# Leading conditioning group in four channel quarters instead of two halves, with four product tiles side by side in a four-layer transformer kernel

## The chip, the cores and the metric

One core of one Trainium2 chip. The metric is the device time of one execution in microseconds (us). The kernel before took 1589.12 us as the median of three runs (1589.05 to 1591.85).

## The reference

Two pairs of transformer layers run on 256 latent tokens (`x`) and 256 context tokens (`ctx`) of width 1024, all in fp32. Only the start matters here:

```python
sh1, sc1, g1, sh2, sc2, g2 = split(silu(c) @ w_ada[0] + b_ada[0], 6)   # the same for c_ctx
h  = rms_norm(x,   norm1_g[0]) * (1 + sc1)  + sh1                      # [256, 1024]
hc = rms_norm(ctx, norm1_g[0]) * (1 + csc1) + csh1                     # [256, 1024]
z, zc = h @ w_in[0], hc @ w_in[0]          # w_in[0]: [1024, 2048]; then attention, MLP, 3 more layers
```

## The kernel before, in words

Activations lie transposed: `X` holds 8 tiles of 128 channels ("k-tiles") by 512 token columns, 0 to 255 latent and 256 to 511 context. A product in fp32 is made of three matmuls on rounded parts: the weight block is split into `WHI` (ScalarE, `hi_split`) and `WLO` (VectorE, `lo_split`), the normalised activations into `HH` (ScalarE, in `norm_hi`) and `HL` (VectorE, `lo` inside `norm`). Weight blocks of 128 outputs by 8 k-tiles (512 KB) come through four `RAW` buffers; block n is in slot n % 4, is loaded when `lo_done` of block n-4 is reached, and is split when `blk_used` frees the slot's halves.

Every engine has its order written out by hand; semaphores join them. What matters is the start of layer 0:

- SyncE's queue loads `CST`, `VEC`, `MOD`, `CV`, `x`, `ctx` and then the first modulation group (`sh1` and `sc1`; 8 MB) into `MW` in six pieces (`PIECES`): two halves of the 1024 channels, each half in pieces of k-tiles 0-3, 4-5, 6-7, with weight blocks 0 to 3 laid between them.
- TensorE, in `first_blocks`, multiplies the conditioning vectors with each piece (`half_units`, line 2019: four matmuls side by side in four 32-column strips of the array), turns the result of a half to channel-major (`turn_half`), and runs product tiles 0 and 1 (`part`): each k-tile of a tile is three matmuls of 512 columns. In the first half it does k-tiles 0 and 1 of tile 0, between the pieces of the second half; the rest comes after the second half.
- VectorE adds a half to `MOD` and derives the scale `DER` (`mod_half`), then writes for each k-tile `NORM` = X * DER * RB (line 1337, two instructions) and `HL` (line 1322, two); ScalarE writes `HH` (line 800) between the two.
- The mean squares of the tokens are made by ScalarE (`first_squares`, one k-tile of 512 columns each) and VectorE (`accumulate`, seven additions), then `acc_sum` on TensorE.
- Tiles 2 and 3 (`products_tok`, weight blocks 2 and 3 side by side, lines 2000 to 2002) keep tokens on the output partitions: two token blocks, 8 k-tiles, three matmuls of 256 columns. They run one after the other in slots 2 and 3 of `proj(0)`. Slots 4 to 15 hold the next 12 tiles.
- The modulation groups 1 and 2 are 16 "units" of 1 MB (`mod_unit`, line 2008), one after each of slots 1 to 16. GpSimd loads them into two buffers, `GWA` and `GWB`, in turn (`unit`), the first two after the last piece of `MW` has landed, each later one when its buffer's last unit has been used.
- `tile_bank` gives tile i the PSUM bank i % 3. ScalarE empties the banks in `proj`, with a table load for Gelu ahead of tile 0's.

Of the kernel before, what the change touches and what calls it, by code (L numbers as in the profile page):

```python
# [161 lines left out]
def build(nc, A):  # L162
    ctx = ExitStack()
    with ctx:
# [48 lines left out]
        MW = sb("MW", [P, 2, KT, 4, 256], at=w0)  # L213
# [56 lines left out]
        vec_in, cst_in, x_in, ctx2_in, lam_in = sem("vec_in"), sem("cst_in"), sem("x_in"), sem("ctx2_in"), sem("lam_in")  # L270
        tab_in = [sem(f"tab_in{l}") for l in range(NLAYER)]
        raw_ready = [sem(f"raw_ready{s}") for s in range(4)]
        hi_done, lo_done, blk_used, drained = sem("hi_done"), sem("lo_done"), sem("blk_used"), sem("drained")
        mw_ready = [sem(f"mw_ready{c}") for c in range(6)]
        half_mm, half_ev, half_turn, half_add = sem("half_mm"), sem("half_ev"), sem("half_turn"), sem("half_add")
# [170 lines left out]
        def tile_bank(l, i):  # L446


            if IS_L[l] and i >= TPROJ[l] - 2:
                return banks[3 if i == TPROJ[l] - 2 else 2]  # L450
            return banks[i % 3]
# [74 lines left out]
        PIECES = [(0, 0, 4), (0, 4, 6), (0, 6, 8), (1, 0, 4), (1, 4, 6), (1, 6, 8)]  # L526
# [5 lines left out]
        def _(sp):  # L532
            sp.dma_start(CST[:], A["cst"]).then_inc(cst_in, 16)
            sp.dma_start(VEC[:], A["vec"]).then_inc(vec_in, 16)
            sp.dma_start(MOD[:].rearrange("p a b -> p (a b)"), A["bmod"]).then_inc(vec_in, 16)
            sp.dma_start(CV[:, 0:4 * KT], A["cvec"]).then_inc(cst_in, 16)
            sp.dma_start(X[:, :, 0:256], A["x"].rearrange("p (k t) -> p k t", k=KT)).then_inc(x_in, 16)
            sp.dma_start(X[:, :, 256:512], A["ctx"].rearrange("p (k t) -> p k t", k=KT)).then_inc(x_in, 16)
# [20 lines left out]
            for l in range(NLAYER):  # L559
                if l < 3:  # L560
                    base = sum(NPROJ[:l])
                    if l == 0:

                        for c, (h, k0, k1) in enumerate(PIECES):
                            r = 2 * h + k0 // 4
                            sp.dma_start(MW[:, h, k0:k1].rearrange("p a b c -> p (a b c)"),
                                         A["wmod0"][P * r:P * r + P, 1024 * (k0 % 4):1024 * (k0 % 4 + k1 - k0)]
                                         ).then_inc(mw_ready[c], 16)
                            for s in ([], [], [0], [1], [], [2, 3])[c]:
                                load(0, s, A["wproj"][s * P:s * P + P, :], 8)  # L570
# [26 lines left out]
        def _(gp):  # L597
# [71 lines left out]
            gp.wait_ge(mw_ready[5], 16)  # L669
# [48 lines left out]
        def _(act):  # L718
# [20 lines left out]
            def row_half(h):  # L739

                if h:
                    act.wait_ge(gb_done, 1)
                    act.wait_ge(half_turn, 1)
                else:
                    act.wait_ge(half_mm, 1)
                act_f(ROW[:, 256 * h:256 * h + 256], GB[:, 0:256], ACT.Copy).then_inc(gb_ev if h else half_ev, 1)

            def first_squares(kt):

                if kt == 0:  # L750
                    act.wait_ge(x_in, 32)
                if kt > 2:
                    act.wait_ge(acc_done, kt - 2)
                act_f(SQ[:, kt % 2, :] if kt else ACC[:], X[:, kt, :], ACT.Square).then_inc(acc_sq, 1)
# [33 lines left out]
            def norm_hi(key):  # L788
# [4 lines left out]
                for kt in range(KT):  # L793
                    if key == (0, "n1") and kt == 4:
                        hi_split(0, 1, 8)
                        row_half(1)
# [53 lines left out]
            def proj(l):  # L850
# [3 lines left out]
                for i in range(NSLOT[l]):  # L854
# [52 lines left out]
                    if (l, i) in ((0, 8), (0, 16)):  # L907
                        row_out({(0, 8): 1, (0, 16): 2}[l, i])
# [253 lines left out]
            for kt in range(KT):  # L1162
                first_squares(kt)
            roots((0, "n1"))
            hi_split(0, 0, 8)
            row_half(0)
            for l in range(NLAYER):
                norm((l, "n1"))
                if l == 0:
                    for s in (2, 3):  # L1170
                        hi_split(0, s, 8)
# [28 lines left out]
        def _(dve):  # L1200
# [28 lines left out]
            def mod_half(h):  # L1229


                dve.wait_ge(sel_done if h else half_turn, 1)
                t = MODP[:, 0:256].rearrange("p (q a b r) -> p a b q r", q=2, a=2, b=2)
                for part in range(2):
                    m = MOD[:, 8 * part + 4 * h:8 * part + 4 * h + 4, :].rearrange("p (b q) c -> p b q c", q=2)
                    ins = v.tensor_tensor(m, m, t[:, part, :, :, 0:2], ALU.add)
                ins.then_inc(mod_add if h else half_add, 1)
                dve.wait_ge(mod_add if h else half_add, 1)
                k = slice(4 * h, 4 * h + 4)
                link(v.scalar_tensor_tensor(out=DER[:, 0, k], in0=MOD[:, 8 + 4 * h:12 + 4 * h, :], scalar=1.0,  # L1240
                                            in1=vec(0, "g1", 4 * h, 4).unsqueeze(2).broadcast_to((P, 4, 2)),
                                            op0=ALU.add, op1=ALU.mult))

# [21 lines left out]
            def norm(key):  # L1265
# [61 lines left out]
                for kt in range(KT):  # L1327
                    if key == (0, "n1") and kt % 4 == 0:
                        if kt:
                            lo(3)  # L1330
                            lo_split(0, 1, 8)
                        mod_half(kt // 4)
# [8 lines left out]
                    if kt and not (key == (0, "n1") and kt == 4):  # L1341
                        lo(kt - 1)
# [36 lines left out]
            def proj(l):  # L1379
# [42 lines left out]
                for i in range(NSLOT[l]):  # L1422
# [33 lines left out]
                    if (l, i) == (0, 11):  # L1456
# [176 lines left out]
            def accumulate(l, which, m, a):  # L1633

                r, t = norm_after(l, which) if which else (0, 512)
# [283 lines left out]
            dve.wait_ge(vec_in, 32)  # L1919
            v.tensor_tensor(vec(3, "bpool", 0, KT), vec(3, "bpool", 0, KT), vec(3, "pscale", 0, KT), ALU.mult)  # L1920
            link(v.tensor_tensor(LPM[:], LP[:, :, 0:4:2, :], LP[:, :, 1:4:2, :], ALU.mult))
            for l in range(2):
                v.tensor_reduce(LAM[:, l, 0:2], LPM[:, l], AX.X, ALU.add).then_inc(lam_dots, 1)
            for l in range(2):
# [10 lines left out]
            for kt in range(1, KT):  # L1935
                accumulate(0, None, kt, kt % 2)
            roots(0, 4)
            lo_split(0, 0, 8)
            for l in range(NLAYER):
# [3 lines left out]
                if l == 0:  # L1943
                    for s in (2, 3):
                        lo_split(0, s, 8)
# [14 lines left out]
        def _(pe):  # L1960
# [31 lines left out]
            def products_tok(s, blocks, bank, qs):  # L1992

                w = P * blocks
                for j, q in enumerate(qs):
                    cols = slice(P * q, P * q + P)
                    out = bank[:, w * j:w * j + w].rearrange("p (a b) -> p a b", b=P)
                    for k in range(8):
                        wh, wl = WHI[:, s:s + blocks, k, :], WLO[:, s:s + blocks, k, :]
                        mm(out, HH[:, k, cols], wh, start=k == 0, stop=False)  # L2000
                        mm(out, HH[:, k, cols], wl, start=False, stop=False)
                        ins = mm(out, HL[:, k, cols], wh, start=False, stop=k == 7)
# [9 lines left out]
            def half_units(c):  # L2012


                h, k0, k1 = PIECES[c]
                pe.wait_ge(mw_ready[c], 16)
                for kt in range(k0, k1):
                    for j in range(4):
                        ins = mm(GB[32 * j:32 * j + 32, 0:256], CV[:, 4 * kt:4 * kt + 32], MW[:, h, kt, j, :],
                                 start=kt == 0, stop=kt == 7)  # L2020
                return ins

            def turn_half(h):

                pe.wait_ge(gb_ev if h else half_ev, 1)
                if h:
                    pe.wait_ge(half_add, 1)
                for q in range(2):
                    c = 256 * h + P * q
                    ins = nc.tensor.transpose(MODP[:, P * q:P * q + P], ROW[:, c:c + P], ident)  # L2030
                ins.then_inc(sel_done if h else half_turn, 1)

            def first_blocks():


                def part(b, ks, ready=None):
                    pe.wait_ge(lo_done, b + 1)
                    return products(b, 8, banks[b], 512, first=ks[0] == 0, stop=ks[-1] == 7, ready=ready, ks=ks)

                pe.wait_ge(cv_ready, 2)  # L2040
                half_units(0)
                acc_sum(0, 512)
                half_units(1)
                half_units(2).then_inc(half_mm, 1)
                norm_spread(0, 4)
                turn_half(0)
                half_units(3)
                part(0, [0, 1], (nl_ready, 0))
                half_units(4)
                half_units(5).then_inc(gb_done, 1)  # L2050
                turn_half(1)
                part(0, [2, 3], (nl_ready, 0))
                part(1, [0, 1, 2, 3])
                for k in range(4, 8):
                    for b in (0, 1):
                        ins = part(b, [k], (nl_ready, 0))
# [670 lines left out]
```

## Time and profile before

| | us |
|---|---|
| median of three runs | 1589.12 |
| the profiled execution | 1590.45 |
| its span, first to last instruction | 1588.4 |
| TensorE matmul busy | 1517.3 |
| TensorE's first matmul starts | 17.97 |
| first matmul of tile 4 starts | 62.40 |

The span is 2.05 us shorter than the profiled execution's time. In the timeline, PE is TensorE, PEld its weight loads, DVE VectorE, ACT ScalarE, POOL GpSimd and SPq the queue of SyncE. A matmul's duration holds its latency, so the distance between two starts says what one costs in a stream. A matmul on plain fp32 operands with 32 weight columns stands as two records.

### The profile page before, as it was taken

What the parts mean: (1) busy time and instruction counts of PE and PEld (TensorE: products, weight loads), DVE (VectorE), ACT (ScalarE), POOL (GpSimd) and SP (SyncE); (2) the same over time, 40 slices, a digit from 0 to 9 for tenths busy, and PEclk for the clock granted to TensorE, in tenths of its full rate; (3) what the DMA queues carried; (4) which work ended last, traced back from release to release, by engine and by line L of the source; (5) the groups of instructions that cost most, each with busy time, mean ns of one, the idle gap of its engine ahead of it and who ended that gap; (6) DMA issues with size and microseconds to landing.
All of it is one profiled execution on the core that took longest, in us unless ns stands there. A gap on an engine that the chain in (4) does not pass through costs nothing. (4 is left out here: it accounts for less than half of the span.)

```text
span 1588.4 us, 27175 instructions
## 1 busy us (share of the span) xinstructions
PE 1517.3 (96%) x9444; PEld 1268.4 (80%) x9444; DVE 1105.1 (70%) x1986; ACT 837.8 (53%) x1526; POOL 94.8 (6%) x160
## 2 busy tenths in 40 slices
PE   4999989999999999899899999999999998799997
PEld 2777667688888888887789998998788886488886
DVE  4464874798786477786678876774678855788865
ACT  3442882544444322465656665546566644566653
POOL 0111000110000011020000000000000000000000
PEclk9999999999999999999999999999999999899999
DMA  9775105665632488452067555542756587445563
GB/s 377 273 234 196 41 2 212 218 225 184 206 119 83 167 262 284 128 156 82 30 260 270 185 148 156 180 126 102 289 160 186 177 302 272 175 131 186 178 186 113
DMA packets 79685, 288.27 MB, mean 181 GB/s; under 512 B 9280, under 2 KB 12864, under 8 KB 71664
## 3 DMA queue, kind: packets, MB, share of 16 engines
q1 hardware_dynamic: 61056, 190.23, 37.8%
q0 software_dynamic: 18544, 96.90, 17.0%
q8 instruction: 54, 0.88, 0.2%
q14 instruction: 31, 0.25, 0.1%
HBM read 283.16 MB, written 1.05 MB: 179 GB/s over the span
## 5 line engine op out<-in xcount | busy, mean ns | idle before, releaser
L1213 DVE TENSOR_TENSOR WLO<-RAW,WHI 128x1024 fp32r<-128x1024 f32 (+1 forms) x376 | 412.2, 1101 | 154.3 <-ACT WHI L726 153.9
L726 ACT ACTIVATE WHI<-RAW 128x1024 fp32r<-128x1024 f32 (+1 forms) x376 | 357.0, 957 | 141.8 <-PE B L1973 86.5
L1971 PE MATMUL B<-HHL,WHI 128*128 128x256 f32 (+1 forms) x1184 | 397.8, 336 | 8.7 <-DVE HHL L1886 3.4
L1972 PE MATMUL B<-HHL,WHI 128*128 128x256 f32 (+1 forms) x1184 | 392.0, 331 | 0.0
L1973 PE MATMUL B<-HHL,WLO 128*128 128x256 f32 (+1 forms) x1184 | 391.9, 331 | 0.0
L1971 PEld LDWEIGHTS B<-HHL,WHI 128*128 128x128 f32 x1184 | 225.5, 190 | 42.2 <-issue 16.7
L1988 PE MATMUL B<-HHL,WHI 128*128 128x512 f32 x704 | 244.2, 400 | 1.7 <-DVE HHL L1322 1.7
L1973 PEld LDWEIGHTS B<-HHL,WLO 128*128 128x128 f32 x1184 | 225.6, 191 | 21.2
L1972 PEld LDWEIGHTS B<-HHL,WHI 128*128 128x128 f32 x1184 | 225.8, 191 | 19.6
L1986 PE MATMUL B<-HHL,WLO 128*128 128x256 f32 x704 | 184.4, 282 | 0.0
L1988 PE MATMUL B<-MID,WHI 128*128 128x512 f32 x462 | 163.5, 400 | 4.3 <-DVE WLO L1213 4.2
L1988 PEld LDWEIGHTS B<-HHL,WHI 128*128 128x128 f32 x704 | 127.7, 190 | 28.3 <-issue 3.8
L1986 PEld LDWEIGHTS B<-HHL,WLO 128*128 128x128 f32 x704 | 133.9, 190 | 8.0
L1986 PE MATMUL B<-MID,WLO 128*128 128x256 f32 x462 | 126.1, 280 | 0.0
L1988 PEld LDWEIGHTS B<-MID,WHI 128*128 128x128 f32 x462 | 85.7, 188 | 26.7 <-DVE WLO L1213 6.0
L1679 DVE SCALAR_TENSOR_TENSOR Y<-B,VEC,Y 128x510 f32<-128x510 f32 (+1 forms) x88 | 54.0, 614 | 57.7 <-ACT Y L1074 45.8
L1971 PE MATMUL B<-MID,WHI 128*128 128x512 f32 (+1 forms) x264 | 91.3, 346 | 0.5 <-DVE WLO L1213 0.5
L1972 PE MATMUL B<-MID,WHI 128*128 128x512 f32 (+1 forms) x264 | 91.0, 345 | 0.0
L1973 PE MATMUL B<-MID,WLO 128*128 128x512 f32 (+1 forms) x264 | 91.0, 345 | 0.0
L1067 ACT ACTIVATE Y<-Y 128x256 f32<-128x256 f32 (+1 forms) x88 | 41.5, 472 | 90.0 <-DVE Y L1704 47.1
L1986 PEld LDWEIGHTS B<-MID,WLO 128*128 128x128 f32 x462 | 87.2, 189 | 1.8
L1078 ACT ACTIVATE MID<-Y 128x256 f32 (+3 forms) x88 | 41.5, 472 | 82.8 <-DVE Y L1722 53.4
(266 smaller groups left out, 2183.4 us busy)
## 6 DMA issues: line engine op xcount, KB each, us to landing
RAW<-in_wup SPq DMA_DIRECT2D x176, 512.0 KB, 3.7
GWR<-in_wmod POOLq DMA_DIRECT2D x27, 1024.0 KB, 8.0
RAW<-in_wdn SPq DMA_DIRECT2D x64, 384.0 KB, 3.2
RAW<-in_wproj SPq DMA_DIRECT2D x44, 512.0 KB, 4.6
RAW<-in_wdn SPq DMA_DIRECT2D x64, 320.0 KB, 3.2
WDU<-in_wdot POOLq DMA_DIRECT2D x32, 512.0 KB, 5.0
WDD<-in_wdot POOLq DMA_DIRECT2D x32, 512.0 KB, 4.8
GWA<-in_wmod POOLq DMA_DIRECT2D x15, 1024.0 KB, 5.9
```

The costliest lines, as they stand in the source:

```text
L726: act_f(WH[s][:, 0:kts, :], RAW[s][:, 0:kts, :], ACT.Copy).then_inc(hi_done, 1)
L1067: act_f(yg, yg, ACT.Silu).then_inc(silu_done, 1)
L1078: act_f(mid, yv if isinstance(i, int) else Y[:, 2 * j + 1:2 * j + 2, 0:t], ACT.Copy).then_inc(mid_hi, 1)
L1213: v.tensor_tensor(WL[s][:, 0:kts, :], RAW[s][:, 0:kts, :], WH[s][:, 0:kts, :].bitcast(F32), ALU.subtract).then_inc(lo_done, 1)
L1679: v.scalar_tensor_tensor(out=y[:, :, 1:256], in0=b[:, :, 0:255], scalar=w(0, which), in1=y[:, :, 1:256], op0=ALU.mult, op1=ALU.add).then_i ...
L1971: mm(bank[:, 0:t], wh, a, start=first and k == ks[0], stop=False)
L1972: mm(bank[:, 0:t], wh, b, start=False, stop=False)
L1973: ins = mm(bank[:, 0:t], wl, a, start=False, stop=stop and k == ks[-1])
L1986: ins = mm(bank[:, 0:256], WL[s][:, k, :], T[:, 0, k0 + k, 0:256], start=False, stop=False)
L1988: ins = mm(bank[:].rearrange("p (a b) -> p a b", a=2), WH[s][:, k, :], T[:, :, k0 + k, 0:256], start=first and k == 0, stop=end)
```

## The change

The first group comes in four quarters of 256 channels (two k-tiles), each in two pieces of 1 MB; weight blocks 0 to 3 are all loaded after the first quarter. `x` and `ctx` move ahead of `VEC` and `MOD`, each with a semaphore of its own, and are squared and added per half of the tokens. All four tiles are open at once (tile 3 in bank 3): each quarter's two k-tiles are multiplied into all four. Units 0 and 1 of group 1 move behind tile 3, units 2 to 13 follow slots 4 to 15, and units 14 and 15 stand in slot 16. The diff, cut to its core:

```diff
-        PIECES = [(0, 0, 4), (0, 4, 6), (0, 6, 8), (1, 0, 4), (1, 4, 6), (1, 6, 8)]
+        PIECES = [(c // 2, 4 * (c % 2)) for c in range(8)]
 # SyncE: CST, CV, X latent (x_in), X context (ctx_in), VEC, MOD, then
-                            for s in ([], [], [0], [1], [], [2, 3])[c]:
+                            for s in range(4) if c == 1 else ():
                                 load(0, s, A["wproj"][s * P:s * P + P, :], 8)
 # GpSimd
-                    if l == 0 and 1 <= i < 15:
-                        unit(1 + (i + 1) // 8, (i + 1) % 8)
+                    if l == 0 and 2 <= i < 16:
+                        unit(1 + i // 8, i % 8)
-            gp.wait_ge(mw_ready[5], 16)
+            gp.wait_ge(mw_ready[7], 16)
 # ScalarE
+            def row_part(q):
+                act.wait_ge(part_mm, q + 1)
+                if q:
+                    act.wait_ge(part_turn, q)
+                act_f(ROW[:, P * q:P * q + P], GB[:, 0:P], ACT.Copy).then_inc(gb_ev if q == 3 else part_ev, 1)
+            def first_squares(n):
+                half, c = n // 4, n % 4
+                j = 3 * half + c - 1
+                if c == 0:
+                    act.wait_ge(ctx_in if half else x_in, 16)
+                elif j >= 2:
+                    act.wait_ge(acc_done, j - 1)
+                out = Y[:, 2 + half, :] if c == 0 else Y[:, j % 2, :]
+                act_f(out..., X[:, 2 * c:2 * c + 2, 256 * half:256 * half + 256], ACT.Square).then_inc(acc_sq, 1)
 # norm_hi
+                    if key == (0, "n1") and kt in (2, 4, 6):
+                        row_part(kt // 2)
                     act.wait_ge(nt_ready, base + kt + 1)
 ...
+                    if key == (0, "n1") and kt == 1:
+                        for s in (1, 2, 3):
+                            hi_split(0, s, 8)
 # before norm:
+            row_part(0)
             hi_split(0, 0, 8)
-            row_half(0)
 # VectorE
+            def mod_part(q):
+                dve.wait_ge(sel_done if q == 3 else part_turn, 1 if q == 3 else q + 1)
+                ... v.tensor_tensor(m, m, t, ALU.add); wait; DER[:, 0, 2q:2q+2] as in mod_half
+            def first_sums(half):
+                acc = Y[:, 2 + half, :]
+                for c in range(1, 4):
+                    ... v.tensor_tensor(acc, acc, Y[:, j % 2, :], ALU.add).then_inc(acc_done, 1)
+                ins = v.tensor_tensor(acc[:, 0:256], acc[:, 0:256], acc[:, 256:512], ALU.add)
 # norm
-                    if key == (0, "n1") and kt % 4 == 0:
+                    if key == (0, "n1") and kt % 2 == 0:
                         if kt:
-                            lo(3)
-                            lo_split(0, 1, 8)
-                        mod_half(kt // 4)
+                            lo(kt - 1)
+                        for s in (1, 2, 3) if kt == 2 else ():
+                            lo_split(0, s, 8)
+                        mod_part(kt // 2)
+                        if kt == 0:
+                            lo_split(0, 0, 8)
 # TensorE
+            def part_units(q):
+                if q:
+                    pe.wait_ge(part_ev, q)
+                for c in (2 * q, 2 * q + 1):
+                    pe.wait_ge(mw_ready[c], 16)
+                    for kt in range(PIECES[c][1], PIECES[c][1] + 4):
+                        for j in range(4):
+                            ins = mm(GB[32 * j:32 * j + 32, 0:P], CV[:, 4 * kt:4 * kt + 32], MW[:, q, kt, j, :],
+                                     start=kt == 0, stop=kt == 7)
+                ins.then_inc(part_mm, 1)
 # first_blocks; wide(b, k): k-tile k of tile b, after lo_done b+1 and nl_ready k+1;
 # tok(tile, k): the same for tiles 2 and 3, after lo_done 4; both(k): wide(0, k), wide(1, k)
+                pe.wait_ge(acc_done, 7); ...four sums of the squares
+                part_units(0); norm_spread(0, 4); turn_part(0)
+                wide(0, 0); wide(0, 1); wide(1, 0); wide(1, 1)
+                part_units(1); tok(2, 0); tok(2, 1); turn_part(1)
+                tok(3, 0); tok(3, 1); both(2); both(3)
+                part_units(2); tok(2, 2); turn_part(2)
+                tok(2, 3); tok(3, 2); tok(3, 3); both(4)
+                part_units(3); both(5); turn_part(3)
+                tok(2, 4); tok(3, 4); tok(2, 5); tok(3, 5)
+                both(6); both(7); tok(2, 6); tok(2, 7); tok(3, 6); tok(3, 7)
 # proj
-                    if l == 0 and 1 <= i < 17:
-                        mod_unit(1 + (i - 1) // 8, (i - 1) % 8)
+                    if l == 0:
+                        for u in (0, 1) if i == 3 else (14, 15) if i == 16 else [i - 2] if i > 3 else ():
+                            mod_unit(1 + u // 8, u % 8)
```

The turn of group 1 and what follows it move one slot later (`row_out`, `mod_turn`, `mod_apply`).

## Rows read from the trace of the kernel before

**Rows 1.** Page, part 1: busy us (share of the span) xinstructions.
```profile
PE 1517.3 (96%) x9444; PEld 1268.4 (80%) x9444; DVE 1105.1 (70%) x1986; ACT 837.8 (53%) x1526; POOL 94.8 (6%) x160
```
**Rows 2.** Waits, 0 to 45 us: us in total, times, longest.
```profile
PE B L2019 <- DMA MW<-in_wmod: 21.1, 2, 18.0
```
**Rows 3.** DMA issues at 37 and 62 us: count, KB each, us to landing.
```profile
GWA<-in_wmod POOLq DMA_DIRECT2D x1, 1024.0 KB, 8.2
...
GWA<-in_wmod POOLq DMA_DIRECT2D x1, 1024.0 KB, 5.2
```
**Rows 4.** Timeline, 12 to 48 us: start, us, engine, line, operation [idle before].
```profile
12.97 0.63 ACT L754 ACTIVATE ACC<-X 128x512 f32<-128x512 f32 x1 [5.67 <-DMA X<-in_ctx]
...
14.24 5.47 DVE L1639 TENSOR_TENSOR ACC<-ACC,SQ 128x512 f32<-128x512 f32 x7 [5.58 <-ACT SQ L754]
...
17.97 3.46 PE L2019 MATMUL B<-MW,CV 128*32 128x256 f32 x32 [17.97 <-DMA MW<-in_wmod]
...
21.36 1.05 PE L2087 MATMUL B<-CST,ACC 128*128 128x1 f32 x8
...
22.34 1.93 PE L2019 MATMUL B<-MW,CV 128*32 128x256 f32 x32
...
46.51 1.28 ACT L881 ACT_TABLE_LOAD   x1
47.81 0.60 ACT L881 ACTIVATE AU<-B 128x512 f32<-128x512 f32 x1
```
**Rows 5.** Timeline, 25 to 30 us, from the row copy to the second half's units.
```profile
25.07 0.36 ACT L746 ACTIVATE ROW<-B 128x256 f32<-128x256 f32 x1
25.27 1.23 DVE L1213 TENSOR_TENSOR WLO<-RAW,WHI 128x1024 fp32r<-128x1024 f32 x1 [2.35 <-ACT WHI L726]
25.49 0.44 PE L2030 MATMUL B<-CST,ROW 128*128 128x128 f32 x2 [0.64 <-ACT ROW L746]
26.41 0.23 DVE L1236 TENSOR_TENSOR MOD<-MOD,B 128x8 f32<-128x8 f32 x2
...
26.87 1.66 DVE L1337 SCALAR_TENSOR_TENSOR NORM<-X,DER,B 128x256 f32<-128x256 f32 x4
...
28.72 0.88 DVE L1322 SCALAR_TENSOR_TENSOR HHL<-NORM,MOD,HHL 128x256 fp32r<-128x256 f32 x2 [0.19 <-ACT HHL L800]
...
29.04 3.64 PE L2019 MATMUL B<-MW,CV 128*32 128x256 f32 x32 [3.11 <-DMA MW<-in_wmod]
```
**Rows 6.** Timeline of TensorE, 46 to 63 us: starts of products and units.
```profile
46.07 0.39 PE L1971 MATMUL B<-HHL,WHI 128*128 128x512 f32 x1
...
46.75 0.39 PE L1971 MATMUL B<-HHL,WHI 128*128 128x512 f32 x1
...
47.52 1.07 PE L2008 MATMUL B<-GWA,CV 128*32 128x512 f32 x8
48.52 0.39 PE L2000 MATMUL B<-WHI,HHL 128*128 128x256 f32 x1
...
54.47 1.06 PE L2008 MATMUL B<-GWB,CV 128*32 128x512 f32 x8
...
62.40 0.50 PE L1971 MATMUL B<-HHL,WHI 128*128 128x512 f32 x1
```
**Rows 7.** The same timeline at 144 us: two strips, 128 columns, 8 pairs.
```profile
144.07 1.09 PE L2183 MATMUL B<-WST,AV 128*64 128x128 f32 x16
```
**Rows 8.** TensorE by stretch: window, us, busy (x), granted clock, DMA share, GB/s.
```profile
28.00:29.00 1.00, 0.00 (x0) 0.50 1.08 446
...
34.00:35.00 1.00, 1.00 (x4) 0.62 0.98 397
...
713.00:714.00 1.00, 0.42 (x2) 1.00 0.69 254
714.00:715.00 1.00, 1.00 (x5) 0.51 0.83 318
```
**Rows 9.** Waits of TensorE, 660 to 720 us: us in total, times, longest.
```profile
PE B L2000 <- DVE WLO L1213: 3.4, 2, 1.9
```

More of the change, by code:

```diff
@@ L273, in build @@
         hi_done, lo_done, blk_used, drained = sem("hi_done"), sem("lo_done"), sem("blk_used"), sem("drained")
-        mw_ready = [sem(f"mw_ready{c}") for c in range(6)]
-        half_mm, half_ev, half_turn, half_add = sem("half_mm"), sem("half_ev"), sem("half_turn"), sem("half_add")
+        mw_ready = [sem(f"mw_ready{c}") for c in range(8)]
+        part_mm, part_ev, part_turn, part_add = sem("part_mm"), sem("part_ev"), sem("part_turn"), sem("part_add")
         gw_ready = {k: sem(f"gw_ready_{k}") for k in GW}
@@ L562, in _ @@
                     if l == 0:
[L564 to L568, printed above, removed]
[L569 removed]
+                        for c, (q, k0) in enumerate(PIECES):
+                            sp.dma_start(MW[:, q, k0:k0 + 4].rearrange("p a b c -> p (a b c)"),
+                                         A["wmod0"][P * q:P * q + P, 512 * k0:512 * k0 + 2048]).then_inc(mw_ready[c], 16)
+                            for s in range(4) if c == 1 else ():
                                 load(0, s, A["wproj"][s * P:s * P + P, :], 8)
@@ L737, in row_out @@
                 act_f(ROW[:], GB[:], ACT.Copy).then_inc(gb_ev, 1)
[L739 to L754, printed above, removed]
+            def row_part(q):
[11 more added lines that the diff above has]
+                out = Y[:, 2 + half, :] if c == 0 else Y[:, j % 2, :]
+                act_f(out.rearrange("p (a b) -> p a b", a=2), X[:, 2 * c:2 * c + 2, 256 * half:256 * half + 256],
+                      ACT.Square).then_inc(acc_sq, 1)
             def late_squares(key, c):
@@ L1161, in _ @@
                 act_f(LAM[:, l, 0:2], LAM[:, l, 0:2], ACT.Exp).then_inc(lam_exp, 1)
-            for kt in range(KT):
-                first_squares(kt)
+            for n in range(8):
+                first_squares(n)
             roots((0, "n1"))
+            row_part(0)
             hi_split(0, 0, 8)
-            row_half(0)
             for l in range(NLAYER):
                 norm((l, "n1"))
-                if l == 0:
-                    for s in (2, 3):
-                        hi_split(0, s, 8)
                 if l < 3:
@@ L1227, in mod_apply @@
                 dve.wait_ge(mod_add, turn_place(g) + 1)
[L1229 to L1241, printed above, removed]
-                                            op0=ALU.add, op1=ALU.mult))
+            def mod_part(q):
+                dve.wait_ge(sel_done if q == 3 else part_turn, 1 if q == 3 else q + 1)
+                m = MOD[:, 0:16, :].rearrange("p (a k) c -> p a k c", a=2)[:, :, 2 * q:2 * q + 2, :]
+                t = MODP[:, 0:P].rearrange("p (a e r) -> p a e r", a=2, e=2)[:, :, :, 0:2]
+                v.tensor_tensor(m, m, t, ALU.add).then_inc(mod_add if q == 3 else part_add, 1)
+                dve.wait_ge(mod_add if q == 3 else part_add, 1 if q == 3 else q + 1)
+                link(v.scalar_tensor_tensor(out=DER[:, 0, 2 * q:2 * q + 2], in0=MOD[:, 8 + 2 * q:10 + 2 * q, :], scalar=1.0,
+                                            in1=vec(0, "g1", 2 * q, 2).unsqueeze(2).broadcast_to((P, 2, 2)),
+                                            op0=ALU.add, op1=ALU.mult))
@@ new lines, in first_sums @@
+            def first_sums(half):
+                acc = Y[:, 2 + half, :]
+                for c in range(1, 4):
+                    j = 3 * half + c - 1
+                    dve.wait_ge(acc_sq, 4 * half + c + 1)
+                    if j:
+                        dve.wait_ge(acc_done, j)
+                    v.tensor_tensor(acc, acc, Y[:, j % 2, :], ALU.add).then_inc(acc_done, 1)
+                dve.wait_ge(acc_done, 3 * half + 3)
+                ins = v.tensor_tensor(acc[:, 0:256], acc[:, 0:256], acc[:, 256:512], ALU.add)
+                if half:
+                    ins.then_inc(acc_done, 1)
+                else:
+                    link(ins)
@@ L1340, in norm @@
                     ins.then_inc(nt_ready, 1)
-                    if kt and not (key == (0, "n1") and kt == 4):
+                    if kt and not (key == (0, "n1") and kt % 2 == 0):
                         lo(kt - 1)
@@ L1633, in accumulate @@
             def accumulate(l, which, m, a):
-                r, t = norm_after(l, which) if which else (0, 512)
+                r, t = norm_after(l, which)
                 dve.wait_ge(acc_sq, 8 * EARLY[r] + m + 1)
@@ L1923, in _ @@
                 v.tensor_reduce(LAM[:, l, 0:2], LPM[:, l], AX.X, ALU.add).then_inc(lam_dots, 1)
+            for half in range(2):
+                first_sums(half)
+            dve.wait_ge(vec_in, 32)
+            v.tensor_tensor(vec(3, "bpool", 0, KT), vec(3, "bpool", 0, KT), vec(3, "pscale", 0, KT), ALU.mult)
             for l in range(2):
@@ L1934, in _ @@
             dve.wait_ge(lam_ready, 2)
-            for kt in range(1, KT):
-                accumulate(0, None, kt, kt % 2)
             roots(0, 4)
-            lo_split(0, 0, 8)
             for l in range(NLAYER):
@@ L1990, in products_apart, with products_tok @@
                 return ins
-            def products_tok(s, blocks, bank, qs):
+            def products_tok(s, blocks, bank, qs, ks=None):
                 w = P * blocks
@@ L1997, in products_tok @@
                     out = bank[:, w * j:w * j + w].rearrange("p (a b) -> p a b", b=P)
-                    for k in range(8):
+                    for k in ks or range(KT):
                         wh, wl = WHI[:, s:s + blocks, k, :], WLO[:, s:s + blocks, k, :]
-                        mm(out, HH[:, k, cols], wh, start=k == 0, stop=False)
-                        mm(out, HH[:, k, cols], wl, start=False, stop=False)
-                        ins = mm(out, HL[:, k, cols], wh, start=False, stop=k == 7)
+                        mm(out, HH[:, k, cols], wh, start=k == 0 and not (ks and j), stop=False, skip_group_check=bool(ks))
+                        mm(out, HH[:, k, cols], wl, start=False, stop=False, skip_group_check=bool(ks))
+                        ins = mm(out, HL[:, k, cols], wh, start=False, stop=k == 7, skip_group_check=bool(ks))
                 return ins
@@ L2010, in mod_kt @@
                 return ins
[L2012 to L2031, printed above, removed]
+            def part_units(q):
[8 more added lines that the diff above has]
+                ins.then_inc(part_mm, 1)
@@ L2033, in first_blocks, with turn_part, wide @@
+            def turn_part(q):
+                if q == 3:
+                    pe.wait_ge(gb_ev, 1)
+                else:
+                    pe.wait_ge(part_ev, q + 1)
+                if q:
+                    pe.wait_ge(part_add, q)
+                nc.tensor.transpose(MODP[:, 0:P], ROW[:, P * q:P * q + P], ident).then_inc(
+                    sel_done if q == 3 else part_turn, 1)
             def first_blocks():
-                def part(b, ks, ready=None):
+                def wide(b, k):
@@ L2050, in first_blocks @@
[L2050 to L2056, printed above, removed]
-                        if k == 7:
-                            ins.then_inc(blk_used, 1)
+                    ins = products(b, 8, banks[b], 512, first=k == 0, stop=k == 7, ready=(nl_ready, 0), ks=[k])
@@ new lines, in wide, with tok, both @@
+                    if k == 7:
+                        ins.then_inc(blk_used, 1)
+                def tok(tile, k):
+                    T = TILES[0][tile]
+                    pe.wait_ge(lo_done, 4)
+                    pe.wait_ge(nl_ready, k + 1)
+                    ins = products_tok(2, 2, tile_bank(0, tile), T["qs"], ks=[k])
+                    if k == 7:
+                        ins.then_inc(*((blk_used, 2) if T["last"] else (tile_mm, 1)))
+                def both(k):
+                    wide(0, k)
+                    wide(1, k)
@@ new lines, in first_blocks @@
+                pe.wait_ge(cv_ready, 2)
+                pe.wait_ge(acc_done, 7)
+                for q in range(4):
+                    ins = mm(STAT[:, q:q + 1], Y[:, 2 + q // 2, P * (q % 2):P * (q % 2) + P], cst("ones"), start=True,
+                             stop=True)
+                ins.then_inc(stat_mm, 1)
+                part_units(0)
+                norm_spread(0, 4)
+                turn_part(0)
+                for b in range(2):
+                    for k in range(2):
+                        wide(b, k)
@@ new lines, in first_blocks @@
+                part_units(1)
+                tok(2, 0)
+                tok(2, 1)
+                turn_part(1)
+                tok(3, 0)
+                tok(3, 1)
+                both(2)
+                both(3)
+                part_units(2)
+                tok(2, 2)
+                turn_part(2)
+                tok(2, 3)
+                tok(3, 2)
+                tok(3, 3)
+                both(4)
+                part_units(3)
+                both(5)
+                turn_part(3)
+                for k in (4, 5):
+                    tok(2, k)
+                    tok(3, k)
@@ L2060, in mod_unit @@
+                for k in (6, 7):
+                    both(k)
+                for tile in (2, 3):
+                    for k in (6, 7):
+                        tok(tile, k)
             def mod_unit(g, kt):
@@ L2210, in proj @@
                         pair()
-                    if 2 <= i < TPROJ[l] - IS_L[l] or l == 2 and i == 1:
+                    if (2 if l else 4) <= i < TPROJ[l] - IS_L[l] or l == 2 and i == 1:
                         tile = 2 if l == 2 and i == 1 else i
```

38 lines of the change are left out of this document (11 added, 27 removed).

## The prediction, on record before the changed kernel ran

> **What bounds the kernel now.** I read the page's first part, then TensorE's waits, then the timeline of the first 65 us. TensorE is busy 96% of the span [rows 1], and the change touches only its start: what matters is when the tile of slot 4 begins, and how much unit work is behind TensorE by then. From there to the weave it waits for nothing but one row copy, and every slot keeps its order. At the start TensorE waits 21.1 us for pieces of `MW` in two waits [rows 2]: 18.0 us for the first, then 3.1 us for the second half, which arrives at 29.04 [rows 5]. In the second wait the clock falls to 0.50, the lower level of 1.2 GHz; it is back between 34 and 35 us [rows 8]. After that the stretch to 62.40 is nearly solid, with three units (0, 1, 2) in it [rows 6]. So 62.40 is the mark: the change gains or loses what the same work ends earlier or later than that.
>
> **What the pieces cost.** Three numbers come first.
> A product's k-tile in tiles 0 and 1 costs 46.75 - 46.07 = 0.68 us [rows 6]; at half clock 1.36. In tiles 2 and 3 it costs (54.47 - 48.52 - 0.2) / 8 = 0.72 us; the 0.2 is the gap ahead of the unit. Interleaving the four tiles adds no instruction: 2 x 8 x 0.68 + 2 x 8 x 0.72 = 22.4 us either way.
> The conditioning product of a quarter has 32 matmuls of 128 columns, where a half had 32 of 256: twice as many in all. Before, 32 records (16 matmuls, eight groups of four strips) took 1.93 us, latency of the last included, so about 0.22 us a group [rows 4]. The 128-column form with 32-column strips does not stand in the trace. Two-strip groups of 128 columns do: eight pairs in 1.09 us, or (1.09 - 0.2) / 8 = 0.11 us a pair [rows 7]. If the time goes with the columns streamed, a quarter is 16 groups x 0.11 = 1.8 us; if with the records, as in that row, 64 x 1.09 / 16 = 4.4 us. I take 1.8, since both rows give half the time for half the columns; at half clock it is 3.6. The upper end would add 2.6 us for each quarter behind the first.
> The Trainium skill (TensorE: Matmul & The Clock Gate, "Back-to-back issue gap") says that pairs of weight load and matmul at N = 128 sustain only about 81 ns each, which would be 5.2 us a quarter and 10 us more for the three; the row of before stands at 54 ns a record and that of two strips at 68, so the trace does not bear it out.
>
> **Until the first product.** The first quarter is 2 MB in the queue's same place as the first piece before, so it is there at about 17.9 [rows 4]. `ctx` was there at 12.97 [rows 4]; 0.53 MB of `VEC` and `MOD` leave its way, at 400 GB/s 1.3 us, so 11.6. Behind it ScalarE squares (0.6 each), VectorE adds three times 0.78 (5.47 / 7) and folds for 0.5: 15.5; sums on TensorE 1.05, so 16.6. The units' first half fills 16.6 to 18.4 at half clock, as the first 32 records did (3.46 against 1.93) [rows 4], the second half ends at 20.2. That the squares come first is thus worth little: TensorE would be free to start at 17.9 in any case. Then the chain: row copy 0.36, turn 0.4, which with the spread ahead of it makes 21.5; `mod_part` 0.46 (26.41 to 26.87); `lo_split` of block 0, which now stands between `mod_part` and the norms, 1.23; norms of two k-tiles 1.66; the wait for ScalarE 0.19 and the first `HL` 0.88 [rows 5]. First product at 25.9 or 26.0, where it was 32.6. The weight blocks (2 MB) are in by 23.
> TensorE idles 4.5 us before it, longer than the 3.1 after which it went to 0.50 before, so I let it be at 0.50 from here for the four wide k-tiles.
>
> **The four quarters on TensorE.** Each quarter has a chain of its own: turn ended, `mod_part` 0.46, norms 1.66, 0.19, `HL` 0.88: 3.2 us to the next product that can run. Beside it TensorE has what the order puts behind the turn.
> - Four wide k-tiles at half clock, 5.4: 31.4. Units of quarter 1, 1.8: 33.2. Two tok 1.44, turn 0.2: 34.9. Behind the turn only tile 3's two k-tiles, 1.44: 36.3. Chain: 35.1 + 3.2 = 38.3. Stall 2.0.
> - Four wide 2.7: 41.0. Units 1.8: 42.8. One tok, turn: 43.8. Three tok 2.16: 45.9. Chain: 44.0 + 3.2 = 47.2. Stall 1.3.
> - Two wide 1.36, units 1.8, two wide 1.36, turn: 51.9. Four tok 2.9: 54.8. Chain 55.3. Stall 0.5.
> - Four wide 2.7, four tok 2.9: 60.9. Units 0 and 1 of group 1, 2.07 (47.52 to 48.52 is one) [rows 6]: 63.0. Slot 4 starts.
> The three `lo_split` of blocks 1 to 3 (26.9 to 30.5) fit beside the first four wide tiles and the units. The last piece of 9 MB lands near 38, before its units at 48.5, so DMA no longer binds from 26 on.
> Slot 4's own wait: block 4 can be split once tile 0 ends at 57.5. ScalarE has its table 1.28 behind it, Gelu 0.60 [rows 4], hi 1.0, VectorE 1.23 [rows 5]: 60.5. The four tok and two units cover it to 63.0; without them it would cost 2.4.
> **The sum.** Before, three units were done at 62.40; now two at 63.0, and the third (1.0) is still due in slot 16, where nothing hides it: 63.0 + 1.0 - 62.4 = +1.6 us. The 14 units left do the same work as before. Unit 2's load is issued when unit 0 has used the buffer, at 62.1, and is needed after slot 4's product at 68.5: 6.4 us, against landings of 5.2 to 8.2 [rows 3]: 0 to +1.8, I take 0, since the long one stood in the crowded start. The squares' seven adds, now six and two folds, lie beside the DMA; one turn more in four, and DER in quarters, are in the chains above. The profiled execution would be 1590.45 + 1.6 = 1592.1 (span 1590.0); on the median of 1589.12 the same shift gives **1590.7**.
>
> **The rivals.**
> *The clock falls in a stall* (slower). TensorE now has gaps of 2.0 and 1.3 us among narrow unit matmuls. Elsewhere a microsecond at 0.42 busy was followed by one at 0.51 of the clock [rows 8], yet a wait of 1.9 us was not [rows 9]. The fall at the start lasted from 28 to past 34, 6.6 us [rows 8], which costs 3.3; one half as long costs 1.7, and I take that. One fall gives +3.3, 1592.4; with unit 2's load late by 1.8 as well, +5.1, 1594.2. It decides when one falls and the sum is not too high elsewhere.
> *Quarters fully hidden* (faster). If the 3.2 us chain lay wholly beside products, the stalls (3.8) go: -2.2; and if the clock also rises before the first wide tiles, -2.7 more: -4.9, 1584.2. For it: TensorE has products to do 6.6 us earlier. Against it: the order puts 1.4 us behind the first turn, and VectorE's instructions are known rows.
> *Only the clock is better.* It rises 2 to 3 us earlier than I let it: 1590.7 - 1.3 = 1589.4, no change that can be told.
> *The narrow matmuls don't halve.* 3 x 2.6 = +7.8, less what the stalls take up of it (nothing, as the chain starts behind them): 1598.5. Against it [rows 4, 7].
> *The change does nothing in effect*, as a gain at the start is lost at slot 4: that is within the forecast.
>
> **How the numbers follow.** A measurement of this kernel can tell about 0.2%, 3.2 us: faster is under 1585.9, slower over 1592.3. My forecast, with the clock case beside it, holds 0.50 (all no change). Clock fall, alone or with the late unit: 0.27, nearly all of it just over the bound. Narrow matmuls: 0.05. Quarters hidden, wholly or with a start chain shorter than I have it: 0.18, of which 0.15 pass the bound. That makes faster 0.15, same 0.53, slower 0.32. The range runs from 1587.0 (half of the stalls hidden, clock up early) to 1594.5 (one fall and a late unit).
>
> **What would show it.** Right: first product (line of `wide`) near 26; waits of TensorE on `HL` of about 2.0, 1.3 and 0.5 us, and no wait for `MW` after the first quarter; a quarter's 64 records in about 1.9 us; slot 4 near 63.0; everything after it shifted by the same amount. Wrong: a slot 4 start before 60 (stalls absent or clock up), a granted clock of 0.50 again between 36 and 50, a wait for `GWA` after slot 4, or a quarter over 3 us.

## The result, and the profile after

The changed kernel takes 1600.83 us (median of six runs, 1596.18 to 1602.78) against 1589.7 for the kernel before in the same runs: ratio 1.0065, interval 1.0051 to 1.008. A forecast of +1.6 us met +11.1. The profiled execution took 1600.62 us, its span 1598.5.

The rows of after stand in the order of the forecast's steps. The page's first part, for [rows 1]:
```profile
PE 1524.4 (95%) x9572; PEld 1277.9 (80%) x9572; DVE 1105.6 (69%) x1989; ACT 837.5 (52%) x1528; POOL 94.8 (6%) x160
```
TensorE is busy for 7.1 us more and the span is 10.1 longer, so part of the loss stands in matmuls (128 records more, and slower ones) and part is waiting. The waits of TensorE in the first 75 us (us in total, times, longest), where [rows 2] had 21.1 us for `MW`:
```profile
PE B L2074 <- DVE Y L1253: 14.9, 1, 14.9
PE B L1985 <- DVE HHL L1337: 8.0, 4, 4.5
PE B L2022 <- DMA GWA<-in_wmod: 1.8, 1, 1.8
```
No wait for `MW` is left. L2074 makes the sums of the squares, and L2022 is a unit. L1985 is the first matmul of a wide k-tile (one of tiles 0 or 1, 512 columns), and its four waits are the gap ahead of the first product and the three stalls. The last line is unit 2, whose load took nearly as long as the crowded one of [rows 3]:
```profile
GWA<-in_wmod POOLq DMA_DIRECT2D x1, 1024.0 KB, 7.9
```
The timeline of the same stretch (L2035 is a quarter's units):
```profile
14.90 1.84 PE L2074 MATMUL B<-CST,Y 128*128 128x1 f32 x8 [14.90 <-DVE Y L1253]
16.67 3.64 PE L2035 MATMUL B<-MW,CV 128*32 128x128 f32 x64
...
22.07 1.23 DVE L1214 TENSOR_TENSOR WLO<-RAW,WHI 128x1024 fp32r<-128x1024 f32 x1
23.21 1.65 DVE L1355 SCALAR_TENSOR_TENSOR NORM<-X,DER,B 128x256 f32<-128x256 f32 x4
...
26.09 0.77 PE L1985 MATMUL B<-HHL,WHI 128*128 128x512 f32 x1 [4.51 <-DVE HHL L1337]
...
31.48 2.21 PE L2035 MATMUL B<-MW,CV 128*32 128x128 f32 x64
...
38.73 0.63 PE L1985 MATMUL B<-HHL,WHI 128*128 128x512 f32 x1 [1.88 <-DVE HHL L1337]
...
43.23 1.95 PE L2035 MATMUL B<-MW,CV 128*32 128x128 f32 x64
...
49.52 0.47 PE L1985 MATMUL B<-HHL,WHI 128*128 128x512 f32 x1 [1.17 <-DVE HHL L1337]
...
58.04 0.47 PE L1985 MATMUL B<-HHL,WHI 128*128 128x512 f32 x1 [0.45 <-DVE HHL L1337]
...
65.66 0.50 PE L1985 MATMUL B<-HHL,WHI 128*128 128x512 f32 x1
...
73.17 1.06 PE L2022 MATMUL B<-GWA,CV 128*32 128x512 f32 x8 [1.78 <-DMA GWA<-in_wmod]
```
The first product is at 26.1 (forecast 26.0), the stalls are 1.9, 1.2 and 0.45 us (2.0, 1.3, 0.5), and a quarter of units at full clock takes 1.95 with its latency. The product behind the first stall shows the main thing that differs up to here: it is slow. TensorE by stretch (window, us, busy, granted clock, DMA share, GB/s), to set beside [rows 8]:
```profile
37.00:38.00 1.00, 0.00 (x0) 1.00 1.02 406
38.00:39.00 1.00, 0.27 (x1) 0.94 1.03 410
39.00:40.00 1.00, 1.00 (x3) 0.50 1.03 410
...
42.00:43.00 1.00, 1.00 (x5) 0.85 1.02 413
...
160.00:161.00 1.00, 0.00 (x0) 1.00 0.94 295
161.00:162.00 1.00, 0.78 (x8) 0.88 0.95 401
162.00:163.00 1.00, 0.68 (x4) 0.50 0.99 418
```
Beside the stretch that the forecast had, from 25.2 to 32.0 us, the clock is at its lower level (1.2 GHz) twice in the first 175 us: for 3.4 us behind the 1.9 us stall, and for 6.8 us from 161.8 on. What stands ahead of that second fall is slot 16, the place the forecast did not work out. TensorE:
```profile
157.19 1.06 PE L2022 MATMUL B<-GWA,CV 128*32 128x512 f32 x8
161.22 1.46 PE L2022 MATMUL B<-GWB,CV 128*32 128x512 f32 x8 [2.97 <-DMA GWB<-in_wmod]
```
and GpSimd, which issues the load that it waits for:
```profile
155.97 0.53 POOL L604 DMA_DIRECT2D GWB<-in_wmod  x1 [6.46 <-PE B L2022]
```
The load took 5.2 us, and unit 15 could have run at 158.2. Before, the last unit's buffer was free at 143.5, 8.6 us ahead of the unit, which ran with no wait:
```profile
143.88 0.53 POOL L605 DMA_DIRECT2D GWB<-in_wmod  x1 [2.38 <-PE B L2008]
152.09 1.06 PE L2008 MATMUL B<-GWB,CV 128*32 128x512 f32 x8
```

**Where the time went.** VectorE's 376 weight splits have the same order in both kernels, so the difference of their starts shows how late the changed kernel is at each point:

| split of | before, us | after is later by | what lies between |
|---|---|---|---|
| block 7 | 64.2 | 2.4 | |
| block 8 | 70.3 | 3.2 | slot 4 |
| block 9 | 80.2 | 5.1 | the wait for `GWA`, 1.8 |
| block 16 | 134.3 | 5.0 | slots 6 to 13 |
| block 17 | 165.6 | 11.9 | slot 16 and the start of the attention behind it (the weave) |
| the last | 1572.2 | 10.2 | the other layers |

Between blocks 16 and 17 stand the unit more in slot 16 (1.0), the wait (3.0) and the half clock behind it (the remaining 2.9). Of the 1.7 given back later, 1.5 lie between 690 and 747 us, where the clock of before fell [rows 8] and that of the changed kernel did not. Later falls move the difference to and fro: it is 11.6 at 1262 us, 7.9 at 1374 and 10.2 from 1416 on.

### The profile page after: what moved, and what is told of

Read it like the earlier page. It is cut to its first block and busy times, and to the rows that moved or that the text cites. A ratio compares the mean times of both kernels' runs of the same rounds, so it can differ in the third digit from the quotient of the medians.

```text
span 1598.5 us, 27467 instructions
## 1 busy us (share of the span) xinstructions
PE 1524.4 (95%) x9572; PEld 1277.9 (80%) x9572; DVE 1105.6 (69%) x1989; ACT 837.5 (52%) x1528; POOL 94.8 (6%) x160
## 3 DMA queue, kind: packets, MB, share of 16 engines
HBM read 283.16 MB, written 1.05 MB: 178 GB/s over the span
## 5 line engine op out<-in xcount | busy, mean ns | idle before, releaser
L1985 PE MATMUL B<-HHL,WHI 128*128 128x256 f32 (+1 forms) x1184 | 398.3, 336 | 15.6 <-DVE HHL L1337 10.6
L1985 PEld LDWEIGHTS B<-HHL,WHI 128*128 128x128 f32 x1184 | 225.5, 190 | 48.8 <-issue 24.8
L1985 PE MATMUL B<-MID,WHI 128*128 128x512 f32 (+1 forms) x264 | 91.4, 346 | 0.5 <-DVE WLO L1214 0.5
```

What stands on the lines that cost most here:

```text
L1985: mm(bank[:, 0:t], wh, a, start=first and k == ks[0], stop=False)
```

## The experiments

A ratio is against runs of the kernel before that stood beside the kernel's own: 1589.81 for e1 to e4, 1589.39 for e5 to e8, 1590.2 for e9 to e11. Most medians are of 11 or 12 runs, that of e3 of six and that of e8 of five. "Filler" is a row of matmuls of 128 columns whose results nobody reads. "Behind before" is always the difference of the starts of the same weight split in the two profiled executions.

| run | median, us | ratio to before, interval |
|---|---|---|
| e1, units put back | 1590.02 | 1.0008, 0.9993 to 1.0023 |
| e2, before with late units | 1594.13 | 1.0031, 1.0017 to 1.0044 |
| e3, changed, with filler | 1597.38 | 1.0044, 1.0029 to 1.006 |
| e4, quarters one ahead | 1586.65 | 0.9979, 0.9968 to 0.9991 |
| e5, e4 with filler | 1585.96 | 0.9975, 0.9963 to 0.9987 |
| e6, e2 with filler | 1594.44 | 1.0027, 1.0013 to 1.004 |
| e7, e4, tables first | 1589.68 | 0.9999, 0.9984 to 1.0014 |
| e8, changed, again | 1600.24 | 1.006, 1.0038 to 1.0083 |
| e9, e4 and 1.75 us | 1589.62 | 0.9998, 0.9988 to 1.0009 |
| e10, e4 and 3.5 us | 1591.16 | 1.0008, 0.9997 to 1.002 |
| e11, before and 1.75 us | 1591.18 | 1.0008, 0.9998 to 1.0018 |

**e1, the units put back.**
```diff
 # GpSimd, ScalarE, VectorE: loads, row copy and use of the units as in the kernel before
 # first_blocks
                 tok(2, 4); tok(3, 4); tok(2, 5); tok(3, 5)
+                mod_unit(1, 0)
                 both(6); both(7)
+                mod_unit(1, 1)
 # proj
-                    if l == 0:
-                        for u in (0, 1) if i == 3 else (14, 15) if i == 16 else [i - 2] if i > 3 else ():
-                            mod_unit(1 + u // 8, u % 8)
+                    if l == 0 and 3 <= i < 17:
+                        mod_unit(1 + (i - 1) // 8, (i - 1) % 8)
```


> The changed kernel, with the unit schedule of the kernel before: unit 0 behind the last turn, unit 1 behind tiles 0 and 1, unit 2 behind tile 3, then one unit a slot. Theory U (most of the loss is unit loads that come due one slot after they are issued, and the clock fall behind the last of them): the waits for GWA (1.8 us) and GWB (3.0) go, and with them the fall to 0.50 at 162 us (about 3.3) - some 8 us faster than the changed kernel, about 1592 to 1594, 3 us over the kernel before. Rival F (the loss is made in the first 65 us, the rest only passes it on): within 2 us of the changed kernel, 1599 to 1601.


It is 10.8 us faster than the changed kernel (10.2 by e8), more than theory U said; rival F falls. Its waits of TensorE in the first 100 us:
```profile
PE B L2074 <- DVE Y L1253: 14.9, 1, 14.9
PE B L1985 <- DVE HHL L1337: 7.6, 3, 4.5
```
Of the stalls of the quarters, those of 1.89 and 1.17 us are still there and unit 0 fills the third; no buffer is waited for, and the clock does not fall at 162. Nor does it after the 1.9 us stall:
```profile
36.00:37.00 1.00, 0.18 (x2) 1.00 0.99 401
37.00:38.00 1.00, 0.00 (x0) 1.00 1.00 401
38.00:39.00 1.00, 0.94 (x4) 1.00 1.08 430
39.00:40.00 1.00, 1.00 (x6) 1.00 1.03 410
```
So theory U holds for the two waits and the fall behind the second; of the surplus, the traces give 1.7 to the fall at 39 us, which e1's execution does not have, and 0.45 to the third stall. By the weight splits e1 is 1.9 us behind before from 63 to 134 us: that is what the front part of the change costs with no such fall and the third stall filled.

**e2, only the late units.** The kernel before with the lines that e1 takes out, put in.


> The kernel before, with only the unit schedule of the change: units 0 and 1 in slot 3, units 2 to 13 in slots 4 to 15, units 14 and 15 in slot 16, loads and turn of the group to match. Theory U: a wait for GWB of 2 to 3 us in slot 16, one for GWA of 0 to 2 us in slot 4, a clock fall at the weave: +5 to +8 us, 1595 to 1598. Rival F: +0 to +2 us.


+4.3 us, a little under theory U's range; F falls again. Its waits of TensorE, 100 to 175 us:
```profile
PE B L2008 <- DMA GWB<-in_wmod: 3.2, 1, 3.2
```
and the clock is at 0.50 from 154.5 to 161.3. Between blocks 16 and 17 it loses 7.0 us, like the changed kernel (6.9). There was no wait for `GWA` in slot 4; that one stands only in kernels that have the change's front as well (the changed kernel, e3, e8).

**e3, filler in the idle times.**
```diff
+                def warm_pe(n):
+                    for _ in range(n):
+                        mm(STAT[:, 128:256], ident, CST[:, 0:128], start=True, stop=True)
                 turn_part(0)
+                warm_pe(20)
...
+                warm_pe(7)
                 both(2)
...
+                warm_pe(4)
                 both(4)
```


> The changed kernel, with matmuls of 128 columns whose results nobody reads in three of its idle times: 20 ahead of the first product, 7 ahead of k-tile 2, 4 ahead of k-tile 4. Theory C (idle TensorE, not the narrow matmuls, brings the clock down): no 0.50 between 25 and 43 us, slot 4 starts 3 to 4.5 us earlier than its 65.7, and the whole is about that much faster than the changed kernel. Rival (the narrow unit matmuls bring it down): the clock falls as before, and the time is the same or up to 1 us longer.


Theory C holds: no 0.50 between 22 and 158 us, slot 4 at 61.9 instead of 65.7, and 3.4 us less in the median (2.9 by the e8 runs). Slot 4 starts with:
```profile
61.94 0.50 PE L1985 MATMUL B<-HHL,WHI 128*128 128x512 f32 x1
```
Narrow unit matmuls alone did not bring the clock down. The saving holds the half clock ahead of 32 us too, which the forecast had counted in. The wait in slot 16 (2.9) and a fall behind it (3.4 us) stayed.

**e4, each quarter one ahead.**
```diff
 # first_blocks, units as in e1
-                wide(0, 0); wide(0, 1); wide(1, 0); wide(1, 1)
-                part_units(1); tok(2, 0); tok(2, 1); turn_part(1)
-                tok(3, 0); tok(3, 1); both(2); both(3)
-                part_units(2); tok(2, 2); turn_part(2)
-                tok(2, 3); tok(3, 2); tok(3, 3); both(4)
-                part_units(3); both(5); turn_part(3)
+                wide(0, 0); wide(0, 1); part_units(1); wide(1, 0); turn_part(1); wide(1, 1)
+                tok(2, 0); tok(2, 1); tok(3, 0); tok(3, 1)
+                part_units(2); both(2); turn_part(2); both(3)
+                tok(2, 2); tok(2, 3); tok(3, 2); tok(3, 3)
+                part_units(3); both(4); turn_part(3); both(5)
```


> The changed kernel with the unit schedule of before and with each quarter's conditioning matmuls and turn put ahead of the products of the quarter before it, so that its chain through VectorE and ScalarE lies beside products. Theory S (the stalls come from the place of the turn, with only 1.4 to 2.9 us of products behind it against a chain of 3.2): the stalls of about 2.3, 1.2 and 0.5 us go, and so does the clock fall in the first of them (1.9); 5 to 6 us less than with the units alone put back, about 1587 to 1588, which is 1 to 3 us under the kernel before. Rival (VectorE's own work, 3.5 us of weight splits and 3.4 a quarter, is the bound): within 2 us of the version with the units put back.


Theory S holds in kind: the stalls are gone, and only the gap ahead of the first product is left (waits of TensorE, 12 to 100 us):
```profile
PE B L2074 <- DVE Y L1253: 14.9, 1, 14.9
PE B L1985 <- DVE HHL L1337: 4.5, 1, 4.5
```
It is 3.4 us under e1 (the stalls of 3.1 us; there was no fall to save) and 3.2 under the kernel before, with an interval that lies under 1. It beats both kernels, though by less than the 5 to 6 us under e1 that were expected.

**e5, and a filler ahead of the first product** (`warm_pe(16)` behind `turn_part(0)`).


> The version with the units put back and the quarters one ahead, with 16 matmuls of 128 columns (results not read) between the first turn and the first product, where TensorE idles 4.5 us and the clock falls at 24.3 us. Theory C: the clock stays up through the first products, which saves 1.4 us in two wide k-tiles, 1.2 in the units and 0.7 in the next, less up to 0.5 if the filler ends late: 2 to 3 us faster, about 1584. Rival (VectorE's three weight splits from 26.5 to 30 us then bind the second tile): 0 to 1 us.


In the trace the clock stays at 1.00 where e4 has 0.50 from 24.3 to 31.1 (the same window in e5 and in e4):
```profile
28.00:29.00 1.00, 1.00 (x44) 1.00 1.05 434
```
```profile
28.00:29.00 1.00, 1.00 (x10) 0.50 1.03 426
```
and block 8's split is 2.0 us earlier, with no wait for a weight split. The median is 0.7 lower, which is the rival's number, and the intervals can't tell the two kernels apart. The gain is shown for the place, not for the whole.

**e6, filler in the wait of slot 16** of e2: 15 such matmuls between units 14 and 15 (`+` lines in `proj`, line 2243).


> The kernel before with the late unit schedule (4.3 us slower than before in the median), and 15 matmuls of 128 columns whose results nobody reads between units 14 and 15, in the wait for GWB. Theory W (of the 7 us lost in slot 16, 3.2 are the wait, 1.0 the unit, and about 3 the half clock that the wait brings): no fall to 0.50 at 155 us, 2.5 to 3.5 us faster than without the filler, 1590.5 to 1592. Rival (the fall comes from the narrow matmuls of the weave itself): no gain, 1594 to 1595.


The fall at the weave is gone with nothing but the filler added, so the idle time did bring it:
```profile
151.20 3.62 PE L2243 MATMUL B<-CST 128*128 128x128 f32 x30
155.36 1.07 PE L2008 MATMUL B<-GWB,CV 128*32 128x512 f32 x8 [0.55 <-DMA GWB<-in_wmod]
```
Blocks 16 to 17 lose 5.2 us instead of 7.0; it would be about 4.3, but this execution's load took 6.3 us where e2's took 5.5. The median did not follow (1594.44 against 1594.13), and by that number the rival fits: theory W holds for the place and not for the whole time. In the two profiled executions e6 is 2.0 us ahead of e2 at block 17 and 0.4 behind it at the last split: its clock is at half for 34.1 us between 1300 and 1405, that of e2 for 23.9. One execution of each can't say whether that is chance, so why the median stays is open.

**e7, tables first.**
```diff
             sp.dma_start(CST[:], A["cst"]).then_inc(cst_in, 16)
+            ...VEC, MOD
             ...CV, x, ctx
-            ...VEC, MOD
```


> The version with the quarters one ahead, with the load order of before (VEC, MOD and CV ahead of the tokens). Theory: the token sums are late by 1.3 us, the first half of the conditioning matmuls starts that much later, and the second half, which waits for its piece until 17.9 anyway, by 0.9: first product and the whole 0.5 to 1 us later, 1587 to 1588, hardly to be told. Rival (the tokens first matter as much as the rest): 2 us or more.


The base is e4. In the trace the sums start 0.9 us later, the first product 0.65, and block 8 is 0.3 later than in e4. The median is 3.0 higher, the rival's number and far more than the trace's front accounts for; with an interval of about 2.4 us on either side it is inconclusive. In its profiled execution e7 is 0.9 us ahead of e4 at 1330 us and 3.1 behind it at 1416, again with 34.1 us at half clock between 1300 and 1405 against 23.9.

**e8, the changed kernel again.**


> The changed kernel once more, beside the others on this chip. If the fall of the clock at 39 us belongs to the 2 us stall there, it can be missing in one execution and present in another, as the version with the units put back had the same stall of 1.9 us and no fall. Waits for GWA of 1 to 2 us and for GWB of 3 us and the fall at the weave are expected every time; median 1598 to 1602.


All as expected: the same waits (1.89, 1.17, 0.45; `GWA` 1.8, `GWB` 3.0), and the clock falls at 38.4 and 161.3. So with this order it fell behind the first stall in both profiled executions, and with e1's, which is the same up to there, it did not.

**e9, e10, e11, a plain shift.**
```diff
                 for i in range(NSLOT[l]):
+                    if (l, i) == (0, 4):
+                        for _ in range(8):        # 16 in e10
+                            mm(MODP[:, 0:P], ident, CST[:, 0:P], start=True, stop=True)
```


> The version with the quarters one ahead, plus 8 matmuls of 128 columns (results not read; 1.75 us by their rate of 0.22 each) ahead of slot 4, with TensorE at full clock. Everything behind is only shifted. Theory K (all that follows passes a shift on unchanged): 1586.65 + 1.75 = 1588.4, within 0.7. Rival P (the short falls of the clock later in the kernel stand at times of their own, so a shift moves the gaps of 700 to 1400 us in or out of them): the median moves by another amount than 1.75, by up to 3 us.

> The same with 16 such matmuls, a shift of 3.5 us. Theory K: 1586.65 + 3.5 = 1590.1, within 0.7. Rival P: off by up to 3 us, and not in line with the shift of 1.75.

> The kernel before with 8 such matmuls ahead of slot 4, a shift of 1.75 us, about that by which the version with the units put back is late there (1.9), though its median is only 0.2 to 0.3 us over that of before. Theory K: +1.75, 1591.3. Rival P: the shift is given back in part by later falls of the clock, as in that version: 0 to +1 us.


In the traces the shifts stand at block 8 as put in: 1.7, 3.6 and 1.8 us. Each against its own runs of before, the median of e4 moved from -3.2 to -0.6 and +1.0, so by 2.6 and 4.2 where 1.75 and 3.5 were put in; that of before moved by 1.0 where 1.75 was. On medians theory K is good to about 1 us, not to the 0.7 it gave itself. Rival P is not ruled out: with intervals of about 1.7 us on either side, e11's +1.0 fits both. For single executions P is what the traces show: e10's span was 1587.2 and e9's 1589.6, with 1.75 us more work in e10, since e9 had 13.6 us more of half clock behind 600 us.

## Why the prediction was wrong

The time of the first product and the three stalls were right to 0.2 us each. In the first there is some luck: the sums of the squares started at 14.90, where the forecast has 15.5, and took 1.84 us instead of 1.05. The narrow conditioning matmuls take half the time, as forecast (1.8 us a quarter; 1.95 with its latency measured). The Trainium skill (TensorE: Matmul & The Clock Gate, "Back-to-back issue gap") gives about 81 ns a matmul with its weight load at N = 128; 64 records in 1.95 us, 0.2 of latency off, are 27 ns each, or 55 for a matmul of two records, so for strips side by side the measurement lies below it.

The step that failed is in the sum: "the third (1.0) is still due in slot 16, where nothing hides it" and "the 14 units left do the same work as before". The work is the same, but not the distance between a buffer's release and its next use. Two buffers alternate, so unit 15 needs the buffer of unit 13. Unit 13 had moved to the end of slot 15, and slot 16 has no product: 2.3 us lie between the issue of the load (155.97) and the time of use (158.2), and the load needs 5.2. The forecast works out unit 2's margin and not the other place where two units stand together, so it puts this wait at nothing without a reason. The price in the trace was 3.0 for the wait and 2.9 for the half clock behind it, which e6's trace ties to the wait. That the unit schedule is the cause is shown both ways: e2 puts it into the kernel before, with a wait of 3.2, and e1 takes it out.

The rival "the clock falls in a stall", given 0.27 with the late unit, came true in both its parts in the profiled execution (1.7 for the fall, 1.8 for `GWA`), beside the failed step and not in its place. By its own price in the forecast, 1594.2, it would have stayed inside the range. Unit 2's load was issued at 65.20, beside four weight blocks (63.19 to 67.87) and the next unit's load (66.06), and took 7.9 us: the crowded landing, which I had set aside.

The parts: slot 4 starts 3.3 us late (0.6 forecast, 1.7 the fall at 39 us, half of its 3.4; 1.0 are small excesses, such as 1.9 to 2.1 for a quarter's units where I had 1.8, so the front's own sum was 1.0 short); `GWA` 1.8; the unit in slot 16 1.0, its wait 3.0, the fall at the weave 2.9. That is 12.0, where the splits show 11.9, less 1.7 later in the kernel. That e1 came to +0.2 and not to 1.9 in the median lies within its interval (-1.1 to +3.7); its profiled execution also lacks the falls that before has at 714 and 810 us, and is 1.0 ahead of it from 907 us on.

## What to carry to other kernels

When steps that share two buffers are moved, write down for each the release of its buffer, the load's landing time and the use; a step dropped into a slot without work of its own is the one to look at. A stall costs its length and, if the clock falls behind it, up to half of the time until it is back, which was as much again here. Where a median moves by less than 3 us, compare the two traces at the n-th instruction of a kind that both kernels share: that shows where the time goes, and how much of a difference at the end is made far behind the change. Where a chain over slower engines feeds TensorE in pieces, put the next piece's trigger ahead of the current piece's products (e4), not behind them.

## What the runs showed of the hardware

- A wait of 1.9 us in the first 40 us was followed by the lower clock in two executions (after, e8) and not in a third (e1), nor was that of 1.9 us in before [rows 9] (at 664.6 us); one of 2.9 to 3.2 us in slot 16 was followed by it in all four that had it (after, e2, e8 for 6.8 us, e3 for 3.4). The 1.9 us stall brought 3.4 us of it.
- Matmuls of 32 weight columns by 128 on four strips side by side: 27 ns a record, half that of 256 columns (54).
- 1 MB landed in 5.2 to 6.3 us in slot 16, with only the next 1 MB load beside it (after 5.2, e2 5.5, e6 6.3), and in 7.9 beside four weight loads of 512 KB and the next 1 MB.
- Between 1300 and 1405 us the clock was at half for 20.5 us in some executions (before, e3, e11) and for up to 34.1 in others (e6, e7), with the same instructions there.
